# Stick-breaking attention: off-diagonal sums in rounded parts, and a head's diagonal sums issued before the next head's scores

## The reference, cut to what matters

```python
for blk in range(seq // Q_BLOCK):                      # 4 blocks of 128 queries
    ...
    z = jnp.einsum('bhqd,bhkd->bhqk', qb, kb) * scale
    past = s_idx < t_idx
    log_beta = jax.nn.log_sigmoid(z)
    log_1m_beta = jnp.where(past, jax.nn.log_sigmoid(-z), 0.0)
    between = lax.cumsum(log_1m_beta, axis=3, reverse=True) - log_1m_beta
    weights = jnp.where(past, jnp.exp(log_beta + between), 0.0)
    outs.append(jnp.einsum('bhqk,bhkd->bhqd', weights.astype(vb.dtype), vb))
```

## Time and profile before

| | us |
|---|---|
| median of 3 runs | 2378.43 (2377.7 to 2380.6) |
| the profiled execution's own time | 2379.26 |
| its span, first to last instruction | 2377.4 |
| PE busy in the span | 2330.8 (98%) |
| chain of waits: PE's share | 89% |

### The profile page before, as it was taken

The page is one execution under the profiler, slowest core; times in us unless marked ns, Lnnn a source line. Parts: engine busy times, 40 slices in busy tenths (PEclk is TensorE's granted clock), DMA queues, the critical chain, the costliest instruction groups (busy, mean ns, idle before and its releaser), DMA issues.

```text
span 2377.4 us, 36786 instructions
## 1 busy us (share of the span) xinstructions
PE 2330.8 (98%) x14851; PEld 2032.8 (86%) x14851; DVE 1644.8 (69%) x2208; ACT 1064.5 (45%) x1394; POOL 339.0 (14%) x294
## 2 busy tenths in 40 slices
PE   7799999999999999999999999999999999999999
PEld 7688899988886678999878779999888878899987
DVE  8835877746667778777586556999636755799942
ACT  6421544532335725446224443455423544455622
POOL 6402100002002340000224241000122002000000
PEclk9899999999999999999999999999999999999999
DMA  2432333233322133332333324233333212333332
GB/s 58 96 105 89 101 108 104 80 106 102 102 101 67 35 97 88 106 105 84 91 114 97 94 62 120 76 107 88 105 103 127 71 54 72 89 107 107 87 106 85
DMA packets 328910, 219.68 MB, mean 92 GB/s; under 512 B 11253, under 2 KB 319115, under 8 KB 328683
## 3 DMA queue, kind: packets, MB, share of 16 engines
q1 hardware_dynamic: 322362, 208.46, 29.8%
q0 software_dynamic: 3024, 7.90, 1.4%
q10 hardware_dynamic: 3360, 1.02, 0.2%
HBM read 206.59 MB, written 2.10 MB: 88 GB/s over the span
## 4 chain that ended last, share of the span: by engine, by line
PE 89%; DVE 5%; POOL 3%; ACT 2%; issue 1%; SPq 0%; DMA 0%; DVEq 0%; ACTq 0%; POOLq 0%
PE psum L1488 9%; PE psum L1490 9%; PE psum L1489 9%; PE psum L1244 9%; PE psum L1245 9%; PE psum L1246 9%; PE psum L1457 3%; PE psum L1458 3%; PE psum L1459 3%; PE psum L1659 1%; PE psum L1661 1%; PE psum L1660 1%; PE psum L1356 1%; PE psum L1352 1%; PE psum L1353 1%
## 5 line engine op out<-in xcount | busy, mean ns | idle before, releaser
L2249 ACT CAST w_hi<-w_stage 128x2048 fp32r<-128x2048 f32 x118 | 225.6, 1912 | 583.5 <-PE psum L1246 389.8
L3219 DVE TENSOR_TENSOR w_lo<-w_stage,w_hi 128x2048 fp32r<-128x2048 f32 x118 | 281.7, 2387 | 238.7 <-ACT w_hi L2249 238.6
L1488 PE MATMUL psum<-x_sum_hi,w_hi 128*128 128x256 f32 x1088 | 308.0, 283 | 0.0
L1490 PE MATMUL psum<-x_sum_hi,w_lo 128*128 128x256 f32 x1088 | 307.9, 283 | 0.0
L1489 PE MATMUL psum<-x_sum_lo,w_hi 128*128 128x256 f32 x1088 | 307.9, 283 | 0.0
L2319 ACT CAST w_hi<-w_parts 128x1024 fp32r<-128x1024 f32 x204 | 213.4, 1049 | 201.1 <-PE psum L1490 111.1
L3347 DVE TENSOR_TENSOR w_lo<-w_parts,w_hi 128x1024 fp32r<-128x1024 f32 x204 | 248.2, 1219 | 51.3 <-ACT w_hi L2319 50.2
L1488 PE MATMUL psum<-x_hi,w_hi 128*128 128x256 f32 x816 | 230.9, 283 | 0.0
L1489 PE MATMUL psum<-x_lo,w_hi 128*128 128x256 f32 x816 | 230.9, 283 | 0.0
L1490 PE MATMUL psum<-x_hi,w_lo 128*128 128x256 f32 x816 | 230.9, 283 | 0.0
L1244 PE MATMUL psum<-hidden_raw_hi,w_hi 128*128 128x512 f32 x572 | 223.6, 391 | 0.3 <-DVE w_lo L3219 0.3
(11 more groups left out here) (653 smaller groups left out, 5395.7 us busy)
## 6 DMA issues: line engine op xcount, KB each, us to landing
w_stage<-in_ffn_w_down_dram SPq DMA_DIRECT2D x64, 704.0 KB, 4.7
w_parts<-in_ffn_w_gu_dram SPq DMA_DIRECT2D x144, 256.0 KB, 3.5
w_parts<-in_ffn_w_gate_dram SPq DMA_DIRECT2D x64, 256.0 KB, 3.0
w_parts<-in_ffn_w_up_dram SPq DMA_DIRECT2D x64, 256.0 KB, 3.2
w_stage<-in_ev_w_in_dram SPq DMA_DIRECT2D x10, 1024.0 KB, 5.2
w_stage<-in_ssm_w_glu_dram SPq DMA_DIRECT2D x8, 1024.0 KB, 5.6
w_stage<-in_ffn_w_gu_dram SPq DMA_DIRECT2D x8, 1024.0 KB, 5.2
w_stage<-in_sb_w_qkv_dram SPq DMA_DIRECT2D x8, 1024.0 KB, 5.2
```

The lines of the kernel that those rows point to most:

```text
L1488: nc.tensor.matmul(dst, hi, x_hi[:, k, :], start=(start and k == 0), stop=False, skip_group_check=True)
L1490: mm = nc.tensor.matmul(dst, lo, x_hi[:, k, :], start=False, stop=(k == DC // 2 - 1), skip_group_check=True)
L2249: nc.scalar.copy(whi[:, half, :], wst[:, half, :]).then_inc(whi_done, 1)
L3219: V.tensor_tensor(wlo[:, half, :], wst[:, half, :], whi[:, half, :].bitcast(F32), ALU.subtract).then_inc(wlo_done, 1)
```

## The change

The softplus of part 1 is now also split into a rounded high part (DVE) and a low part (POOL), and the sums of part 1 and of the diagonal blocks into later queries all go through rounded matmuls, once for the high and once for the low part. The three block sums on DVE go away, and with them a semaphore; PE adds the single blocks instead. The parts have two buffers each, in the second half of the weight buffers `w_hi` and `w_lo`, so the rounding of w_o's second weight half on ACT moves behind the last head's weights. In PE's list, the triangular sums of head h's diagonal blocks, high and low, now stand in front of the scores of head h+1, and the mix stands between the high and the low sums of part 1. The change of the list of semaphore names is left out.

```diff
--- before.py
+++ after.py
@@ -307,11 +307,12 @@
 
         stick = [at(f"stick{n}", [P, STICK], where) for n, where in enumerate(
             (tmp_at, tmp_at + 5 * KB, tmp_at + 10 * KB, hid_at + 32 * KB, hid_at + 37 * KB, hid_at + 76 * KB))]
-        drop_sum = at("drop_sums", [P, 2, 3 * P], hid_at + 81 * KB)
         neg_up_to = at("neg_up_to", [P, P], hid_at + 84 * KB, F32R)
         neg_ones = at("neg_ones", [P, P], hid_at + 84 * KB + 512, F32R)
-        sp_hi = at("soft_hi", [P, SEQ], hid_at + 42 * KB, F32R)
-        sp_lo = at("soft_lo", [P, SEQ], hid_at + 85 * KB, F32R)
+        OFF = STICK - SEQ
+        soft_own = [(at("soft_own_hi0", [P, SEQ], hid_at + 42 * KB, F32R), at("soft_own_lo0", [P, SEQ], hid_at + 85 * KB, F32R)),
+                    (whi[:, 1, OFF:STICK], wlo[:, 1, OFF:STICK])]
+        soft_off = [(whi[:, 1, 0:OFF], wlo[:, 1, 0:OFF]), (whi[:, 1, STICK:TILE], wlo[:, 1, STICK:TILE])]
         after, _ = new("mask_after", [P, P])
         up_to, _ = new("mask_up_to", [P, P])
         ident_r, _ = new("ident_rounded", [P, P], F32R)
@@ -943,11 +944,12 @@
                 if h + 2 < HEADS:
                     swap_halves(h + 2)
 
-                pool.wait_ge(sp_done, 3 * h + 2)
-                if h >= 1:
-                    pool.wait_ge(cs_done, 2 * (h - 1) + 1)
-                nc.gpsimd.tensor_tensor(sp_lo[:, :], stick[h % 6][:, 0:SEQ], sp_hi[:, :].bitcast(F32),
-                                        ALU.subtract).then_inc(sp_low, 1)
+                for part, (hi, lo) in enumerate((soft_own[h % 2], soft_off[h % 2])):
+                    pool.wait_ge(sp_done, 4 * h + 2 * part + 2)
+                    if h >= 2:
+                        pool.wait_ge(cs_done, 2 * (h - 2) + 2)
+                    nc.gpsimd.tensor_tensor(lo[:, :], stick[h % 6][:, STICK_PARTS[part]], hi[:, :].bitcast(F32),
+                                            ALU.subtract).then_inc(sp_low, 1)
 
             deviation_sums(2)
             deviation_sums(3)
@@ -1712,9 +1714,11 @@
                                  not_past[:, :].unsqueeze(1).to_broadcast([P, TT, P]), start=True, stop=False,
                                  skip_group_check=True)
 
+                own_keys, own_queries = k_f[:, h // 2, :], q_f[:, h // 2, :]
+
                 def own_block(j):
                     block = slice(j * P, (j + 1) * P)
-                    return nc.tensor.matmul(flat[:, block], k_f[own, h // 2, block], q_f[own, h // 2, block], start=False,
+                    return nc.tensor.matmul(flat[:, block], own_keys[own, block], own_queries[own, block], start=False,
                                             stop=True, skip_group_check=True)
 
                 def later_queries(j, rows, keys, queries):
@@ -1730,38 +1734,44 @@
                 own_block(2)
                 later_queries(2, other, k_swap, q_swap)
                 own_block(3).then_inc(z_done, 1)
-                later_queries(1, own, k_f[:, h // 2, :], q_f[:, h // 2, :]).then_inc(z_done, 1)
-
-            def stick_sums(h):
+                later_queries(1, own, own_keys, own_queries).then_inc(z_done, 1)
+
+            def stick_sums(h, between):
 
                 flat = psum[:, 4 * (h % 2):4 * (h % 2) + 3, :].rearrange("p b n -> p (b n)")
-                sp = stick[h % 6]
-                ends = flat[:, 512:1024].rearrange("p (a b) -> p a b", b=P)[:, 0::3, :]
-
-                def own_sums(part):
-                    nc.tensor.matmul(flat[:, 0:SEQ], neg_up_to[:, :], part[:, :], start=False, stop=True, skip_group_check=True)
-
-                def end_sums(part):
-                    return nc.tensor.matmul(ends, neg_ones[:, :], part[:, :].rearrange("p (a b) -> p a b", b=P)[:, 1::2, :],
-                                            start=False, stop=True, skip_group_check=True)
-
-                pe.wait_ge(sp_done, 3 * h + 2)
-                own_sums(sp_hi)
-                pe.wait_ge(sp_done, 3 * h + 3)
-                end_sums(sp_hi)
-                nc.tensor.matmul(flat[:, REST[1]:REST[1] + P], neg_ones[:, :].bitcast(F32), sp[:, 2 * P:3 * P],
-                                 start=False, stop=True, skip_group_check=True)
-                pe.wait_ge(sp_low, 2 + h + 1)
-                own_sums(sp_lo)
-                end_sums(sp_lo).then_inc(cs_done, 1)
-                for c0, c1 in ((512, 1024), (1024, STICK)):
-                    nc.tensor.matmul(flat[:, c0:c1], neg_up_to[:, :].bitcast(F32), sp[:, c0:c1], start=False, stop=True,
-                                     skip_group_check=True)
-                pe.wait_ge(sums_done, 3 * h + 3)
-                for to, c0, c1 in ((REST[1] + P, 2 * P, 3 * P), (REST[0] + P, 0, 2 * P)):
-                    mm = nc.tensor.matmul(flat[:, to:to + c1 - c0], neg_ones[:, :].bitcast(F32), drop_sum[:, h % 2, c0:c1], start=False,
-                                          stop=True, skip_group_check=True)
-                mm.then_inc(cs_done, 1)
+                up, one = neg_up_to[:, :], neg_ones[:, :]
+
+                def add(matrix, to, part, c0, n):
+                    return nc.tensor.matmul(flat[:, to:to + n], matrix, part[:, c0:c0 + n], start=False, stop=True,
+                                            skip_group_check=True)
+
+                def own_ends(part):
+                    add(one, REST[0], part, P, 3 * P)
+                    add(one, REST[1], part, 2 * P, 2 * P)
+                    add(one, REST[2], part, 3 * P, P)
+
+                def off_sums(part):
+                    add(up, SEQ, part, 0, SEQ)
+                    add(up, 2 * SEQ, part, SEQ, STICK - 2 * SEQ)
+                    add(one, REST[0] + P, part, REST[1] - SEQ, 2 * P)
+                    add(one, REST[0] + 2 * P, part, REST[2] - SEQ, P)
+                    return add(one, REST[1] + P, part, REST[2] - SEQ, P)
+
+                (own_hi, own_lo), (off_hi, off_lo) = soft_own[h % 2], soft_off[h % 2]
+                pe.wait_ge(sp_done, 4 * h + 2)
+                add(up, 0, own_hi, 0, SEQ)
+                pe.wait_ge(sp_low, 2 + 2 * h + 1)
+                add(up, 0, own_lo, 0, SEQ).then_inc(cs_done, 1)
+                if h + 1 < HEADS:
+                    stick_scores(h + 1)
+                pe.wait_ge(sp_done, 4 * h + 3)
+                own_ends(own_hi)
+                own_ends(own_lo)
+                pe.wait_ge(sp_done, 4 * h + 4)
+                off_sums(off_hi)
+                between()
+                pe.wait_ge(sp_low, 2 + 2 * h + 2)
+                off_sums(off_lo).then_inc(cs_done, 1)
 
             def stick_mix(p, part):
 
@@ -1788,13 +1798,13 @@
 
                 pe.wait_ge(sp_low, 2)
                 for h in range(HEADS):
-                    if h + 1 < HEADS:
-                        stick_scores(h + 1)
-                    stick_sums(h)
-                    if h == 2:
-                        pe.wait_ge(evac_done, ST["v"].evac1)
-                    if h >= 2:
-                        stick_mix(h // 2 - 1, h % 2)
+                    def mix_before(h=h):
+                        if h == 2:
+                            pe.wait_ge(evac_done, ST["v"].evac1)
+                        if h >= 2:
+                            stick_mix(h // 2 - 1, h % 2)
+
+                    stick_sums(h, mix_before)
 
             def last_mix(k):
 
@@ -2590,7 +2600,6 @@
             def stick_weights(h, part):
 
                 act.wait_ge(cs_done, 2 * h + part + 1)
-                act.wait_ge(sums_done, 3 * h + 3)
                 z = psum[:, 4 * (h % 2):4 * (h % 2) + 3, :].rearrange("p b n -> p (b n)")
                 nc.scalar.activation(stick[h % 6][:, STICK_PARTS[part]], z[:, STICK_PARTS[part]], ACT.Exp).then_inc(w_done, 1)
 
@@ -2707,12 +2716,12 @@
                         stick_exp(h + 1, 0)
                         stick_ln(h + 1, 0)
                         stick_exp(h + 1, 1)
-                    else:
-                        split(st.it0 + st.iters, 1, st.part1)
                     stick_weights(h, 0)
                     if h + 1 < HEADS:
                         stick_ln(h + 1, 1)
                     stick_weights(h, 1)
+                    if h + 1 == HEADS:
+                        split(st.it0 + st.iters, 1, st.part1)
                     if h >= 3 and h % 2 == 1:
                         pair_high(h // 2 - 1)
 
@@ -3917,25 +3926,14 @@
 
                 z = psum[:, 4 * (h % 2):4 * (h % 2) + 3, :].rearrange("p b n -> p (b n)")
                 sp = stick[h % 6]
-                for part in range(2):
+                for part, (hi, _) in enumerate((soft_own[h % 2], soft_off[h % 2])):
+                    columns = STICK_PARTS[part]
                     dve.wait_ge(ln_part, 2 * h + part + 1)
-                    V.scalar_tensor_tensor(sp[:, STICK_PARTS[part]], z[:, STICK_PARTS[part]], 0.0, sp[:, STICK_PARTS[part]],
-                                           ALU.max, ALU.add).then_inc(sp_done, 1)
-                    if part == 0:
-                        dve.wait_ge(sp_done, 3 * h + 1)
```

(22 more changed lines are left out.)

## The result

| | median, us | lowest to highest | runs |
|---|---|---|---|
| before, beside it on the chip | 2379.08 | 2377.7 to 2381.19 | 10 |
| changed | 2384.65 | 2382.39 to 2389.36 | 10 |

The ratio is 1.0027, 95% interval 1.0019 to 1.0034: 5.57 us slower, where the forecast was 5.7 slower. The profiled execution of the changed kernel took 2387.49 us, 2.84 over its median. Its three longest runs, 2387.49 to 2389.36, had a mean granted clock of 0.990 to 0.992, the other seven one of 0.994 to 0.996; why the runs lie so far apart is part of what follows.

A forecast was written before the change was run, and what follows sets the result against it. PE's in-order list bounded the kernel before; a 6.57 us loop through POOL would bound it after. Start +1.37 and clock +1.0, twelve heads +3.49, end -0.15: +5.7 us, 2384.1 us expected, range 2380 to 2388.5.

The forecast's parts named there:

- The bound: PE bounds the kernel before; after the change it works less and idles about 0.7 us a head before the low part.
- The loop: From one head's scores to the next's through POOL's subtraction: 6.57 us a head, against 6.28 before; +3.49 us over twelve heads.
- The 0.34: Loop term on PE: from the start of the matmul POOL releases to the next matmul's start, 0.34 us.
- PE's work: The new sums on PE take 2.61 us instead of 3.06; PE's own pace falls from 6.28 to 5.83 us a head.
- The cover of the other engines: DVE's added rounding (0.64 us) and POOL's added subtraction (1.82 us), both of 768 columns, stay hidden.
- only just no new wait: Last low sums end 5.25 us after the first product in odd iterations, when ACT reaches part 1's weights.
- The signs: PE's low sum waits 0.3 to 0.9 us, products lie 6.5 to 6.65 apart, mid-stage PE busy about nine tenths.
- The start: The first product of head 3 comes at 745.97 instead of 744.60 us: +1.37 us.
- The clock: Falls of PE's clock during waits in the first heads: between 0 and 3.7 us, taken as +1.0.
- Rival 1: The clock at the start stays up, so the +1.0 us goes: 2383.1 us; chance 25%.
- Rival 2: PE doesn't wait for POOL, ACT's loop of 6.10 us bounds: 2377.5 us, no change; chance 15%.
- Rival 3: Narrow matmuls cost 0.22 us, odd heads 0.3 more, DVE's rounding holds up the next abs: 2386 to 2388 us; 20%.

The follow-up runs named there:

- kernel 5: Changed kernel with spare matmuls, four before and four after the high diagonal sum of heads 0 to 2: 2383.43 us, ratio 1.0016.
- kernel 3: Kernel before with only the order changed, both diagonal sums in front of the next head's scores, sums still unrounded: 2384.99 us, ratio 1.0026.
- kernel 4: Changed kernel with the low diagonal made on DVE instead of POOL, which keeps only the low part of part 1: 2378.96 us, ratio 1.0001.
- kernel 8: Changed kernel with POOL's diagonal remainder made twice, one after the other: 2414.24 us, ratio 1.0146.
- kernel 7: Changed kernel with the next head's scores back in front of both diagonal sums and the mix behind the last low sums: 2377.7 us, ratio 0.999.
- kernel 1: Changed kernel with the next head's scores back in front of both diagonal sums, the mix left as changed: 2382.25 us, ratio 1.0014.
- kernel 11: Kernel before with six spare matmuls between the mask and the first score product of heads 2 to 4: 2379.72 us, ratio 1.0004.
- kernel 6: Changed kernel with only the mix moved behind the last low sums of part 1: 2384.54 us, ratio 1.0023.
- kernel 9: kernel 4 (low diagonal on DVE) with the mix moved behind the last sums: 2378.91 us, ratio 1.0002.

## Why the prediction was right

**The bound.** That PE's idle time would decide and not its work was right: in the middle of the stage it works less than before (5.45 to 5.89 of 6 us at full clock, where it was 6.00), and the kernel is slower. The page's sum of PE's busy time hides this, 2333.5 us against 2330.8, since the first heads ran at half clock.

**The loop.** 6.57 predicted, 6.56 by the rows and 6.58 by the pace of heads 5 to 15; every term is within 0.01 of its row. (From head 3 on it is 6.79 in this execution, with the second fall of the clock in it, and 6.58 in kernel 5.) The 0.34, and that L1352 begins only after L1356, were read from weight loads (PEld in the earlier trace rows), which say nothing of the order of matmuls; between matmuls the changed kernel shows the same 0.34 (782.24 to 782.58), and no matmul of the next head starts before the released one. Twelve heads at 6.58 instead of 6.28 are +3.6, predicted +3.49. Kernels 3, 4 and 8 move with this loop as they should: the order alone gives it, a shorter subtraction takes it away, a second one adds 1.34 us a head where the clock stays up.

**PE's work.** This term was too low, without effect on the time. The sums take 2.79 us (kernel 7), not 2.61, still inside the bounds. A narrow matmul takes 0.06 us until the next one starts, its lower bound (changed kernel, 781.08 to 781.14), and 0.11, as was taken, where it is the second of two (781.14 to 781.25); the weight loads there start 0.11 apart as well (781.09 and 781.19). What was missing are gaps: the first sum of kernel 7 takes 0.33 us until the next one starts, where the next takes 0.23, each first sum of part 1 takes 0.28, and from the last narrow one 0.21 pass until the mix. The Trainium skill (TensorE: Matmul & The Clock Gate, section Back-to-back issue gap) gives about 81 ns for a matmul of 128 columns in a stream of weight loads and matmuls, and about 131 ns for one of 512; only the mean of the pair above comes near the first, a single narrow one takes less, and 512 columns take 0.23 us here.

**The cover of the other engines.** POOL's subtraction of 768 columns takes 1.82 us, as predicted, and DVE's rounding 0.56 instead of 0.64 where it stands alone. Both stayed hidden. The "only just no new wait" for ACT's last weights was nearly right (0.21 us at 775.30, which delayed no product), and it was worth more than the text made of it: in kernel 1 that wait is the next bound.

**The signs.** First products lie 6.5 to 6.65 us apart, as was said. The others came out weaker than said: PE is idle in front of the low sum for 0.54 and 0.11 us by turns, not 0.3 to 0.9 in nearly every head, and it is busy for 5.70 of 6 us on average from 759 to 825 us, 95% and not nine tenths. The idle time of about 0.7 us a head was the loop minus PE's work, and that work was priced too low.

**The start.** At full clock (kernel 5) the first products of heads 0 and 3 lie 21.57 us apart, 725.11 and 746.68, against 20.19 in the earlier trace rows: +1.38, predicted +1.37. But both set a start at full clock against an execution of before whose own clock fell (0.75 in the earlier trace rows); from mask to mask of heads 0 and 3 kernel 5 takes 21.57, before 19.26 and kernel 11, before at full clock, 18.19. What the order costs at the start with the same clock on both sides is not separated. The clock was put at +1.0, a choice between 0 and 3.7 that no row made; kernel 5 makes it 1.4 of the median. Rival 1 is in effect that kernel: +4.1 measured, +4.7 computed.

**Rivals 2 and 3** are refuted: PE does wait for POOL, in 11 of the 12 heads from 742 to 822 us, narrow matmuls are not dearer than the forecast's, and DVE stands idle for 0.20 us before the next abs (777.52), so the rounding doesn't hold it up.

**What the sum does not show.** +3.6, +1.4, +1.4 and -0.2 make 6.2 where 5.6 was measured. The paces come from one execution each, and 0.05 us of pace would be the difference; kernel 5's profiled execution alone lies 0.75 above its median. So the mechanism was right, and that the forecast lies within 0.2 us of the measurement is in part luck. What the prediction missed lies outside its question: undoing its one cause does not bring the time back, because the mix stands in front of the last sums.

## What to carry to other kernels

In an in-order list, ask of each wait that is moved forward what stands behind it; if that feeds the next round, sum up the whole round across the engines, from start to start of one instruction, and compare the sum with the pace. Work saved on an engine that then waits is worth nothing. When a loop like this is taken away, look for the next one before counting the gain: two faults of the order were worth 2.2 and 0.3 us when mended singly and 7.2 us together (kernels 1, 6 and 7, each against its own before; the intervals of 1 and 6 overlap with the changed kernel's, so the single sizes are rough). Spare matmuls keep the clock up only for the price of standing on the path wherever the wait is shorter than they are.

## What the hardware showed

- The clock. In the changed kernel's profiled execution it fell to 1.2 GHz after a wait of 1.94 us, and again after two of 0.61 and 0.85 that stood close together; in kernel 8 it fell several times up to the end of the stage, with waits of up to 2.33 us. After the single waits of 0.54 us from 759 us on, in heads that are otherwise full, it did not fall. Whether a fall comes differs from one execution to the next: kernels 4 and 9 have the same work on PE up to their third head, and one had 1.00 and the other 0.72 from 729 to 735 us. With no fall in kernel 5 the runs lie within 1.73 us instead of 6.97, so the falls are most of that spread.
- DVE's rounding beside POOL. The rounding of 768 columns takes 0.56 us alone and 1.24 when it starts at 776.66 beside POOL's subtraction (776.23 to 777.49, kernel 8), so it ends 0.41 us after POOL; POOL, at 1.26, loses nothing. In the changed kernel it took 0.88 from 730.86 and ended 0.42 us after a subtraction that began at 730.05 and took 1.27. In all sixteen heads of kernel 8 it ends 0.41 to 0.42 us after POOL, wherever in POOL's subtraction it began. The softplus of DVE beside POOL kept its 0.96. The Trainium skill (SBUF — State Buffer, section SBUF: two separate sides) calls the ports that DVE and GpSimd share an exclusive lock, which the one that starts first holds for its whole instruction, where DVE's operation needs them; the constant end after POOL's agrees with it. That the rest is 0.41 and not the 0.56 of the whole rounding, no run here explains.
